# A hybrid decoder block on one core: expert gates added by the scatters instead of summed on VectorE

## What is computed

```
q = h @ w_q                                  # 8 heads x 256
s1, s2 = first half of q @ k1, second half of q @ k2      # 128 keys each
v1, i1 = top_k(s1, 16);  v2, i2 = top_k(s2, 16)
top_s, top_j = top_k(v1 + v2 over all 256 pairs, 16)
ids = 128 * i1 + i2 of the 16 chosen pairs   # one of 16384 experts
gates = softmax(top_s)
out = sum over heads and the 16 of: gate * gelu(h . u[id]) * v[id]
```

## Time and profile before

| | before |
|---|---|
| median of 3 runs | 1732.4 us (1731.78 to 1732.47) |
| span of the profiled execution | 1730.8 us |
| own time of the profiled execution | not given beside its span |
| TensorE busy | 1724.4 us (100%) |
| VectorE busy | 1326.9 us (77%) |
| ScalarE busy | 720.8 us (42%) |
| GpSimd busy | 939.5 us (54%) |
| DMA | 363.35 MB, mean 210 GB/s |

### The profile page before, as it was taken

How to read it: one execution, slowest core, us unless ns; L and a number is a source line. 1 busy time by engine, 2 the same in 40 slices (tenths; PEclk the granted TensorE clock), 3 DMA queues, 4 the chain that set the end, 5 groups by cost and what they waited for, 6 DMA issues and landing times.

```text
span 1730.8 us, 25631 instructions
## 1 busy us (share of the span) xinstructions
PE 1724.4 (100%) x9296; PEld 1492.5 (86%) x9296; DVE 1326.9 (77%) x2389; ACT 720.8 (42%) x1116; POOL 939.5 (54%) x743
## 2 busy tenths in 40 slices
PE   9999999999999999999999999999999999999998
PEld 7788888888888888899999999888888888888887
DVE  6566421568799999999999998446888888888874
ACT  7644322443332222344433433444444444444454
POOL 6433344444347777777777777236666666573200
PEclk9999999999999999999999999999999999999999
DMA  6222232348764444245444454769999999999821
GB/s 209 97 74 74 88 133 96 122 165 321 256 227 156 144 147 156 74 158 161 159 159 156 157 162 162 247 212 338 367 370 385 365 378 364 385 370 371 297 85 50
DMA packets 156382, 363.35 MB, mean 210 GB/s; under 512 B 31680, under 2 KB 72640, under 8 KB 156128
## 3 DMA queue, kind: packets, MB, share of 16 engines
q1 hardware_dynamic: 102224, 259.56, 43.5%
q0 software_dynamic: 34816, 67.41, 10.9%
q10 hardware_dynamic: 19216, 34.74, 5.5%
HBM read 300.54 MB, written 61.01 MB: 209 GB/s over the span
## 4 chain that ended last, share of the span: by engine, by line
PE 98%; DVE 1%; ACT 0%; issue 0%; DVEq 0%; POOL 0%; ACTq 0%; POOLq 0%
PE pair L679 18%; PE pair L681 18%; PE pair L680 18%; PE pair L921 18%; PE pair L945 7%; PE pair L944 7%; PE pair L943 7%; PE pair L732 1%; PE pair L797 1%; PE pair L885 1%; PE pair L788 0%; PE pair L740 0%; PE pair L1028 0%; PE pair L819 0%; PE pair L820 0%
## 5 line engine op out<-in xcount | busy, mean ns | idle before, releaser
L633 POOL DMA_INDIRECT gates<-gate_val,gate_at x384 | 443.1, 1154 | 155.2 <-issue 111.7
L603 POOL TENSOR_TENSOR wl<-raw,wh 128x1024 fp32r<-128x1024 f32 x85 | 205.6, 2426 | 288.9 <-ACT wh L1131 277.9
L1131 ACT ACTIVATE wh<-raw 128x1024 fp32r<-128x1024 f32 x266 | 279.2, 1054 | 105.8 <-PE pair L681 86.7
L679 PE MATMUL pair<-wh,act_h 128*128 128x512 f32 x768 | 298.9, 389 | 0.0
L681 PE MATMUL pair<-wh,act_l 128*128 128x512 f32 x768 | 298.8, 389 | 0.0
L680 PE MATMUL pair<-wl,act_h 128*128 128x512 f32 x768 | 298.8, 389 | 0.0
L1805 DVE TENSOR_TENSOR wl<-raw,wh 128x1024 fp32r<-128x1024 f32 x182 | 220.9, 1218 | 42.3 <-ACT wh L1131 41.7
L652 POOL DMA_INDIRECT picked<-score_dram,score_at x128 | 146.0, 1141 | 170.8 <-PE pair L681 111.2
L679 PE MATMUL pair<-hh,wh 128*128 128x512 f32 x456 | 182.2, 400 | 0.0
L659 POOL DMA_INDIRECT rows<-stream,row_at x128 | 140.8, 1100 | 70.7 <-PE pair L681 35.9
L681 PE MATMUL pair<-hh,wl 128*128 128x512 f32 x456 | 178.3, 391 | 0.0
(11 more groups left out here) (303 smaller groups left out, 3510.9 us busy)
## 6 DMA issues: line engine op xcount, KB each, us to landing
raw<-stream SPq DMA_DIRECT2D x337, 512.0 KB, 3.9
score_dram<-gout ACTq DMA_DIRECT2D x128, 256.0 KB, 2.3
gates<-zeros SPq DMA_DIRECT2D x48, 512.0 KB, 6.3
score_in<-score_dram SPq DMA_DIRECT2D x128, 192.0 KB, 6.4
gate<-gates SPq DMA_DIRECT2D x128, 192.0 KB, 7.1
gates<-gate_val,gate_at POOLq DMA_INDIRECT x384
x<-xT SPq DMA_DIRECT2D x7, 512.0 KB, 4.8
picked<-score_dram,score_at POOLq DMA_INDIRECT x128, 5.7
```

The costliest lines, as they stand in the source:

```text
L603: nc.gpsimd.tensor_tensor(wl[:, n % SL, :], raw[:, n % RAW, :], wh[:, n % SL, :].bitcast(F32), ALU.subtract).then_inc(lo_done, 1)
L633: nc.gpsimd.indirect_dma_start(gate_list, bass.IndirectOffsetOnAxis(ap=gate_at[:, r, k:k + 1], axis=0), gate_val[:, r, k:k + 1], None).the ...
L679: nc.tensor.matmul(out, ah, bh, start=start, stop=False)
L1131: nc.scalar.activation(wh[:, n % SL, :], raw[:, n % RAW, :], ACT.Copy).then_inc(hi_done, 1)
```

## The change

VectorE no longer compares experts. A tile's gates go straight into `gate_val`, and its addresses release the whole tile: `gates_ready` now counts tiles. Each scatter adds its value to what is in `gates` instead of writing it, so equal experts add up in DRAM; the waits between heads of one tile stay. The order of heads takes the three tiles in turn as early as it can. The pace of the first 142 scatters is one slope, 8 beats for 13, instead of two slopes. The exponentials stand at units 5, 12, 19 and 26 instead of 5, 17, 30 and 42. The pairs stay at unit 48, and the pace within the pairs stays.

```
-HEAD_ORDER = [(0, 0), (0, 1), (0, 2), (0, 3), (1, 0), (0, 4), (1, 1), (0, 5), (1, 2), (0, 6)]
-HEAD_ORDER += [(2, 0), (1, 3), (0, 7), (2, 1), (1, 4), (2, 2), (1, 5), (2, 3), (1, 6), (2, 4), (1, 7), (2, 5), (2, 6), (2, 7)]
+HEAD_ORDER = [(0, 0), (0, 1), (1, 0), (0, 2), (2, 0), (1, 1), (0, 3), (2, 1), (1, 2), (0, 4), (2, 2), (1, 3), (0, 5), (2, 3)]
+HEAD_ORDER += [(1, 4), (0, 6), (2, 4), (1, 5), (0, 7), (2, 5), (1, 6), (2, 6), (1, 7), (2, 7)]
...
 def pace(i):
-    if i < 65:
+    if i < PLAIN_SCATTERS:
         return 12 + i * 8 // 13
-    if i < PLAIN_SCATTERS:
-        return 52 + (i - 65) * 4 // 7
...
-EXP_AT = (5, 17, 30, 42)
+EXP_AT = (5, 12, 19, 26)
...
-        alone = sb("alone", [P, HK], F32, rs)
-        earlier = sb("earlier", [P, HK], F32, rs)
...
                 if i % TOPK == 0:
-                    pool.wait_ge(gates_ready, PH * r + h + 1)
+                    pool.wait_ge(gates_ready, r + 1)
                     if h > 0:
                         pool.wait_ge(scattered[r], 16 * TOPK * h)
...
                 nc.gpsimd.indirect_dma_start(gate_list, bass.IndirectOffsetOnAxis(ap=gate_at[:, r, k:k + 1], axis=0),
-                                             gate_val[:, r, k:k + 1], None).then_inc(scattered[r], 16)
+                                             gate_val[:, r, k:k + 1], None, compute_op=ALU.add).then_inc(scattered[r], 16)
...
-                mine = alone if tt else pick_g
-                nc.vector.tensor_tensor(mine[:].rearrange("p (h k) -> p h k", h=PH), top[:],
+                mine = gate_val[:, r, :] if tt else pick_g[:]
+                nc.vector.tensor_tensor(mine.rearrange("p (h k) -> p h k", h=PH), top[:],
                                         gsum[:, 0, :].unsqueeze(2).to_broadcast([P, PH, TOPK]),
                                         ALU.mult).then_inc(chosen_ready, 1)
...
-                link(nc.vector.tensor_scalar(gate_at[:, r, :], picked[:], float(DENSE), token[:, tt - 1:tt], ALU.mult, ALU.add))
-                nc.vector.tensor_copy(gate_val[:, r, 0:TOPK], alone[:, 0:TOPK]).then_inc(gates_ready, 1)
-                for h in range(1, PH):
-                    n, own = TOPK * h, slice(TOPK * h, TOPK * (h + 1))
-                    same = cand[:].rearrange("p h a b -> p (h a b)")[:, 0:TOPK * n].rearrange("p (k j) -> p k j", j=n)
-                    link(nc.vector.tensor_tensor(same, picked[:, own].unsqueeze(2).to_broadcast([P, TOPK, n]),
-                                                 picked[:, 0:n].unsqueeze(1).to_broadcast([P, TOPK, n]), ALU.is_equal))
-                    beside(0.1 + 0.02 * n)
-                    link(nc.vector.tensor_tensor(same, same, alone[:, 0:n].unsqueeze(1).to_broadcast([P, TOPK, n]), ALU.mult))
-                    beside(0.1 + 0.02 * n)
-                    link(nc.vector.tensor_reduce(earlier[:, own], same, AX.X, ALU.add))
-                    nc.vector.tensor_tensor(gate_val[:, r, own], alone[:, own], earlier[:, own], ALU.add).then_inc(gates_ready, 1)
-                    beside(0.3 + 0.02 * n)
+                nc.vector.tensor_scalar(gate_at[:, r, :], picked[:], float(DENSE), token[:, tt - 1:tt],
+                                        ALU.mult, ALU.add).then_inc(gates_ready, 1)
```

## The result

The changed kernel takes 1903.56 us (median of 4 runs, 1903.36 to 1904.27) against 1732.43 us: a ratio of 1.0983, with a 95% interval of [1.0967, 1.0999]. The forecast was no change, 1732.4 us, with a range up to 1785 us. Rival (a), GpSimd made slower by the add, is what happened, but with 171 us lost, three times the 53 us at which the range ended.

What follows compares the result with a forecast made beforehand. TensorE, busy 1724.4 of 1730.8 us, was taken to bound the kernel. VectorE's 80.6 us less, head order, tiles, exponentials and add were each worth 0, giving 1732.4 us, range 1729 to 1785 us.

Steps and rivals of the forecast that it cites:

- Rival (a): Scatters on GpSimd: the add slows them and they end past 1110 us; x = 0.2 gives 1754 us; chance 0.33.
- the part on the add: Scatters: the add's price on GpSimd, between 0 and 0.96 us each, taken as 0; its DMA load fits.
- x: Extra us on GpSimd for each adding scatter: taken as 0, upper bound 0.96, TensorE paying from 0.11.
- the prediction's own formula: GpSimd as the bound from the first scatter: 508.6 + 384 x 2.41 = 1434 us, 324 us late, at 0.96 us.
- The rule of two reads: Scatters that add: named in favour of GpSimd getting slower with the add; given no size of its own.
- There was nothing to gain: 468 to 1140 us: TensorE is never held up there, so VectorE's 80.6 us less is worth 0.
- Tiles were ready: Release by whole tiles: addresses ready about 540 and 572 us, ahead of the scatters by 12 and 34 us; cost 0.
- ScalarE didn't stand at an exponential: ScalarE's queue: exponentials' inputs ready 13, 19 and 25 us early, so ScalarE waits for nothing; cost 0.
- VectorE waited for two of them: VectorE in the routing: waits some 2 and 8 us for exponentials, with low parts still in time; cost 0.
- rival b: DMA engines: adds land late or load the engines, so raw units come late; about 1768 us; chance 0.03.
- the point from which TensorE pays: Behind the pairs: the last scatter may end at about 1110 us before TensorE's unit 125 is held up.
- The time for gelu: ScalarE, block 0: gelu may start as late as 1119.8 us before the copy that TensorE's unit 125 needs is late.

Runs made afterwards that it cites:

- experiment 1: The changed kernel with the add taken out, so its scatters write (shared experts keep one head's gate only): 1732.64 us, ratio 1.0004.
- experiment 2: The kernel before with only the add put into its scatters, VectorE still making its sums: 1935.51 us, ratio 1.118.

## Why the prediction was wrong

**The step that failed** is in the part on the add: "the price doesn't follow what is moved, so I take x = 0". It measured x = 0.56 us in the mean (1711 - 1154 ns), 0.59 in the median, well inside the bounds 0 and 0.96 that stood in the same paragraph. The rows used for the choice, gathers against scatters, showed that the two directions cost the same; neither adds, so they said nothing of an add. With both ends that far apart and no row near, the value was a guess, and the multiplication further down (384 instructions on an engine that uses 96% of its pace) should have weighed on the chances: at x = 0.56 the prediction's own formula, 508.6 + 384 x (1.45 + 0.56) = 1280 us, gives the end of the last scatter within 5 us (1283.1 + 1.55), and the loss with it.

**The rule of two reads** was the better guide in direction. The Trainium skill (Collectives: The Full Stack, Stop 4) has two reads for an add, and the Trainium skill (GPSIMD Engine Reference, section 4) has one of two cores writing the read descriptors. The trace agrees that the add makes more of something: software-queue packets rise from 34816 to 77824, 112 more for each scatter, from 32 to 144 of them. But a doubled list would have lost half its surcharge at half the list, and the runs show 467 ns left at 32 entries. Nor does the price follow the packets: an adding scatter of 64 entries makes 80 and one of 32 makes 48 (page totals 53248 and 40960), a writing one 32 whatever its list, so at 32 entries the 112 more packets have shrunk to 16 while four fifths of the surcharge are left. The larger part goes by the instruction, about 0.42 us; this is an estimate by the straight line through the differences of the minima at 32, 64 and 128 entries (455, 521 and 591 ns). What GpSimd does in that time stays open.

**The range.** It stopped at x = 0.33 because a chance of 0.18 for all above seemed small enough. The bound of 0.96 us meant 2056 us; a term that is known only as 0 to 0.96, times 384 on a full engine, is no narrow tail. The 1785 us for x = 0.33 was also too low by the prediction's own rows: it takes scatter 142 as still on its pace at 733.5 us, but 142 scatters of 1.45 + 0.33 us from 508.6 us on end at 761 us. Counted from the first scatter, as was done for x = 0.96, x = 0.33 gives 1192 us for the end, 82 us late and 1814 us in all; 1785 us belongs to x = 0.25.

**What held.** There was nothing to gain: experiment 1 takes 1732.6 us with 77 us less on VectorE. Tiles were ready at 537.92 + 0.34 and 574.22 + 0.35 us (forecast 540 and 572), and ScalarE didn't stand at an exponential. VectorE waited for two of them, 4.1 and 5.7 us (forecast 2 and 8), at no cost:

```profile
573.00 0.29 DVE L1889 TENSOR_REDUCE gsum<-top 128x8 f32<-128x128 f32 x1 [4.12 <-ACT top L1475]
...
611.08 0.29 DVE L1889 TENSOR_REDUCE gsum<-top 128x8 f32<-128x128 f32 x1 [5.70 <-ACT top L1475]
```

The DMA engines took the adds easily (rival b): their share in the pairs went from 0.50 to 0.64, and TensorE stayed full there. That was with ten times the share for the software queue: 16.6% in the pairs' stretch after 1.6%. The landing at i = 16 cost 3.0 us, where experiment 1 without the add has 1.9.

**A size that was off:** the point from which TensorE pays. The prediction had the last scatter's end at 1110 us; it is 1114.5 + 1.5 = 1116 us. Of the 6 us, 4 are the first score block, which landed 2.4 us after its issue and not 6.4, the median of all 128; the rest is SyncE's issue, 1.7 us after the last scatter's end and not about 3. The time for gelu, 1119.8 us, was right (1122.36 - 2.5). And the 2.6 us at TensorE's lower clock behind the gap were not in the price of a stall.

## What to carry to other kernels

An operation that no row shows, on an engine that is nearly full and many times over, is a measurement to make before the design, not a zero: one scatter with the add beside one without would have told 0.96 from 1.55 us. And work taken off an engine that bounds nothing (78 us of VectorE here) is worth no price on an engine that is at 96% of its pace. What feeds the last transfer of a stage has a deadline that can be read (1114.5 us here): ahead of it delay is free, behind it each us is paid in full, so 48 of the dear instructions cost nothing early and a few us late.

## What the runs showed of the hardware

- An indirect scatter of single values that adds into DRAM takes GpSimd 1.55 us for 128 entries, 1.43 for 64 and 1.33 for 32; one that writes takes 0.96, 0.89 and 0.87 us. Between two of them lie 0.30 us either way. So an adding scatter of 32 entries is only 14% cheaper than one of 128.
- The adding form makes 144 packets a transfer in the software queue at 128 entries, 80 at 64 and 48 at 32; the writing one 32 at each of the three.
- Where two heads of one tile follow each other, the second's first scatter waited for the first's landing, 3.0 us with the add and 1.9 us without it at the same place (changed kernel, experiment 1); five such places took 2.1 to 4.2 us with the add (experiment 2) and 1.9 to 3.5 us without (kernel before). With lists of 64 or 32 added it was 2.0 us, with 32 written 3.7. So that an adding transfer lands later isn't settled.
- Both forms are stretched beside a part of VectorE's work: in the pairs' stretch adding ones take 310.57/176 = 1.76 us and, with VectorE idle behind it, 137.57/89 = 1.55 us. By the trace it goes by the instruction that runs beside them, not by VectorE being busy. In experiment 1, where a writing scatter takes 0.96 us, the 33 that had `gout<-pair,gout` beside them for over 70% of their time took 0.954 to 0.962 us, and the 33 that had the low parts `wl<-sums,wh` there took 1.76 us in the mean. One of each sort, from the timelines of GpSimd and VectorE:

```profile
804.32 1.99 POOL L629 DMA_INDIRECT gates<-gate_val,gate_at  x1 [0.88 <-PE pair L941]
803.13 2.35 DVE L1992 TENSOR_TENSOR wl<-sums,wh 128x1024 fp32r<-128x1024 f32 x2
...
809.33 0.96 POOL L629 DMA_INDIRECT gates<-gate_val,gate_at  x1 [0.30 <-issue]
809.30 0.69 DVE L2041 TENSOR_TENSOR gout<-pair,gout 128x512 f32<-128x512 f32 x1
```

  No run here changes that instruction alone, so what in it does this stays open.
- After 169 us without work TensorE's granted clock was at the lower level, and the first unit took 8.02 us instead of 5.44 us.
